# First norm, memory norm and memory keys/values as a lane beside the compression; semaphores cleared in the next block; last stores from two queues

## What is computed

```
u    = rms_norm(x, norm_g[0])                       # 1056 x 1024, input of one large projection (u @ w_in)
mkv  = rms_norm(mem_prompt, mem_norm_g) @ w_mkv     # 256 x 1024 @ 1024 x 512, an output, read later by cross-attention
kc,vc = compress(k, v of the page cache)            # sparse attention: blocks of 32 rows through a small MLP, 8 sequences + the prompt
rms_norm(x, g) = x * rsqrt(mean(x*x) + 1e-6) * g
```

## Time and profile before

| | us |
|---|---|
| three runs | 3834.92, 3834.66, 3845.22 (median 3834.92) |
| the profiled execution, whole | 3842.91 |
| its span in the trace | 3841.1 |
| PE busy | 3306.4 (86%) |
| blocks before the first merged stage (nm, memory_kv, n0) | 0 to 88.2 |
| first merged stage (36 dense units and the compression) | 88.2 to 476.4 |
| mean TensorE clock granted | 0.917 |

### The profile page before, as it was taken

How to read it: one execution, slowest core, us unless ns; L and a number is a source line. 1 busy time by engine, 2 the same in 40 slices (tenths; PEclk the granted TensorE clock), 3 DMA queues, 4 the chain that set the end, 5 groups by cost and what they waited for, 6 DMA issues and landing times. The chain is left out here.

```text
span 3841.1 us, 40240 instructions
## 1 busy us (share of the span) xinstructions
PE 3306.4 (86%) x14082; PEld 2043.6 (53%) x14082; DVE 1115.2 (29%) x2789; ACT 729.8 (19%) x1746; POOL 397.0 (10%) x296
## 2 busy tenths in 40 slices
PE   4799967778999968887999957989869999997998
PEld 2567745555556645544554535545546666663443
DVE  2011101111453315843555523313322232230000
ACT  1011100000221112322333322014411111111000
POOL 0010000000321003411000011001101101100000
PEclk7799988889997879998999978979989999998999
DMA  3333233232774226784001134420011111104000
GB/s 109 89 95 87 61 98 103 79 104 64 221 228 130 82 80 194 259 281 123 30 29 34 42 85 130 144 82 24 28 45 37 41 33 36 41 22 152 23 32 14
DMA packets 340509, 345.19 MB, mean 90 GB/s; under 512 B 54529, under 2 KB 311265, under 8 KB 339126
## 3 DMA queue, kind: packets, MB, share of 16 engines
q1 hardware_dynamic: 330002, 285.16, 24.5%
q10 hardware_dynamic: 10334, 57.82, 4.4%
HBM read 289.57 MB, written 110.01 MB: 104 GB/s over the span
## 5 line engine op out<-in xcount | busy, mean ns | idle before, releaser
L243 PE MATMUL d_ps<-d_w,mixer_u_T 128*128 128x288 f32 (+4 forms) x2304 | 723.9, 451 | 57.9 <-ACT d_ob L263 29.9
L2795 PE MATMUL ffn_ps<-up_u_T,ffn_w 128*128 128x352 f32 x2112 | 632.4, 461 | 0.0
L243 PEld LDWEIGHTS d_ps<-d_w,mixer_u_T 128*128 128x128 f32 (+1 forms) x2304 | 408.6, 192 | 227.3 <-issue 86.0
L2795 PEld LDWEIGHTS ffn_ps<-up_u_T,ffn_w 128*128 128x128 f32 x2112 | 400.4, 190 | 220.2 <-issue 1.2
L247 PE MATMUL d_ps<-mixer_u_T,d_w 128*128 128x352 f32 x1152 | 428.4, 497 | 44.4 <-PEq L86 40.0
L2676 PE MATMUL down_ps<-down_w,feed_g_T 128*128 128x512 f32 (+1 forms) x792 | 343.1, 596 | 17.6 <-DMA down_w<-ffn_w_down 17.6
L247 PEld LDWEIGHTS d_ps<-mixer_u_T,d_w 128*128 128x128 f32 x1152 | 206.6, 199 | 152.9 <-issue 89.2
L2676 PEld LDWEIGHTS down_ps<-down_w,feed_g_T 128*128 128x128 f32 (+1 forms) x792 | 144.4, 183 | 215.8 <-issue 197.9
L263 ACT COPY d_ob<-d_ps 128x288 f32<-128x288 f32 (+3 forms) x144 | 59.8, 417 | 662.6 <-PE d_ps L243 451.0
L2855 DVE TENSOR_SCALAR ffn_c<-ffn_h,ffn_now 128x1072 f32<-128x1072 f32 x44 | 36.9, 838 | 449.3 <-ACT ffn_h L2823 449.3
L2821 ACT COPY ffn_h<-ffn_ps 128x352 f32<-128x352 f32 x132 | 58.6, 444 | 526.7 <-PE ffn_ps L2795 526.7
(11 more groups left out here) (443 smaller groups left out, 3418.4 us busy)
## 6 DMA issues: line engine op xcount, KB each, us to landing
out_dil_sample<-cache_dil_w ACTq DMA_DIRECT2D x8, 4088.0 KB
ffn_w<-ffn_w_up SPq DMA_DIRECT2D x44, 512.0 KB, 4.7
cmp_rows<-cache_nsa_kv SPq DMA_DIRECT2D x128, 128.0 KB
graw<-d_ob SPq DMA_DIRECT2D x72, 176.0 KB, 1.9
mix_gate<-graw SPq DMA_DIRECT2D x24, 528.0 KB, 6.2
dils_qb<-proj SPq DMA_DIRECT2D x24, 512.0 KB, 7.2
d_w<-w_in SPq DMA_DIRECT2D x24, 512.0 KB, 5.6
ssd_x<-proj SPq DMA_DIRECT2D x29, 384.0 KB, 4.7
```

What stands on the lines that cost most here:

```text
L243: mm = pe.matmul(self.ps[u % 2][0:rows, 0:cols], self.u_T[:, k, r0:r0 + rows], self.view(i)[:, k, :], start=(k == 0), stop=(k == DK - 1))
L2795: mm = pe.matmul(ps[u][:, 0:chunk], w[:, slot, k, a, :], u_T[:, k, x * chunk:(x + 1) * chunk], start=(k == 0), stop=(k == DK - 1))
```

## The change

1. The blocks "nm", `memory_kv`, "n0" and the one that loads `ident` go. A new lane, `front_lane`, does their work in the first merged stage: nine tiles of x (F0 to F17, two halves a tile), two tiles of the memory (F18 to F21), and the 16 products of the memory's keys and values (F22 to F37). It has four input buffers and one PSUM bank (before four), so each half of the transposes waits for the copy of the half before. The dense lane waits (`ready`) for the tile that a unit of the first weight part reads.
2. The two output tiles of the compression share one PSUM bank, and the waits around them are for both tiles.
3. `Stage.__exit__` only notes its semaphores; POOL clears them at the beginning of the next block that calls `clear`, before its own work there (all `together` blocks, `combine_branches`, `ffn_up`, `project_out` and the last block; not `merge_branches`).
4. The last stores of nsas and dilp are issued half from SP and half from ACT.
5. The SSD's last states go to a buffer each (`h_raw`, whose content has been used by then, and `last_rows`), with no wait for stores in between.

```
@@ Stage
-        if self.sems and exc[0] is None:
-            with self.nc.Block() as block:
-                @block.gpsimd
-                def _(pool):
-                    for sem in self.sems:
-                        pool.sem_clear(sem)
-            for sem in self.sems:
-                self.nc.release_semaphore(sem)
+        Stage.used += self.sems
+def clear(nc, pool):
+    for sem in Stage.used:
+        pool.sem_clear(sem)
+        nc.release_semaphore(sem)
+    Stage.used = []
@@ together, combine_branches, ffn_up, project_out, last block
             @block.gpsimd
             def _(pool):
+                clear(nc, pool)
@@ Dense.lane, pe_program
                 if j == 0:
                     pe.wait_ge(self.w_in[i % 2], self.landed[i])
+                if ready is not None and i == 0:
+                    pe.wait_ge(ready, 2 * (j + 1))
@@ decoder_step
-            with Stage(nc, "cmp") as own:
-                together(nc, (dense.lane(36), 0, 0.8), (compress_lane(nc, own, ins, proj, kc_T, vc, ident), 0, 1))
+            with Stage(nc, "front") as own_f, Stage(nc, "cmp") as own:
+                normed = own_f.sem("normed")
+                front = front_lane(nc, own_f, ins, outs, u_T, x_rows, ident, ident_in, normed)
+                together(nc, (front, 0, 0.3), (dense.lane(36, ready=normed), 0.03, 0.82),
+                         (compress_lane(nc, own, ins, proj, kc_T, vc, ident), 0, 1))
@@ front_lane (new), its programs; copied is the semaphore "normed"
+    def pe_program(pe):
+        pe.wait_ge(ident_in, 16)
+        pe.wait_ge(gain_in, 32)
...
+        for t, (r0, m, _, _, _) in enumerate(tiles):
+            for j in range(2):
+                pe.wait_ge(scaled, 2 * t + 2)
+                if t or j:
+                    pe.wait_ge(copied, 2 * t + j)
+                for k in range(4):
+                    mm = pe.transpose(ps[:, k, 0:m], xt[0:m, t % RING, (4 * j + k) * P:(4 * j + k + 1) * P], ident[0:m, 0:m])
+                mm.then_inc(turned, 1)
+                yield
+        pe.wait_ge(w_in, 16)
+        pe.wait_ge(copied, 2 * own)
+        for t in range(MEM // P):
+            if t >= 1:
+                pe.wait_ge(kv_copied, t)
+            for k in range(DK):
+                mm = pe.matmul(ps[...], m_T[:, k, t * P:(t + 1) * P], w[:, k, :], start=(k == 0), stop=(k == DK - 1))
...
+    def act_program(act):
+        def root(t):
+            m, s = tiles[t][1], t % 2
+            act.wait_ge(x_in[t % RING], 16 * (t // RING + 1))
...
+            act.activation(junk[0:m, :], xt[0:m, t % RING, :], ACT.Square, accum_out=ss[0:m, 0, s:s + 1]).then_inc(squared, 1)
+            act.wait_ge(meaned, t + 1)
+            act.activation(ss[0:m, 2, s:s + 1], ss[0:m, 1, s:s + 1], ACT.Sqrt).then_inc(rooted, 1)
+        root(0)
+        for t in range(own):
+            if t + 1 < own:
+                root(t + 1)
+            yield
+            yield
+    def dve_program(dve):
+        def scale(t):
...
+            dve.tensor_scalar(xt[0:m, t % RING, :], xt[0:m, t % RING, :], ss[0:m, 3, s:s + 1], None, ALU.mult).then_inc(scaled, 1)
...
+        scale(0)
+        for t, (r0, m, _, out_T, g) in enumerate(tiles):
+            if t + 1 < own:
+                scale(t + 1)
+            for j in range(2):
+                dve.wait_ge(turned, 2 * t + j + 1)
+                dve.tensor_tensor(out_T[:, 4 * j:4 * j + 4, r0:r0 + m], ps[:, :, 0:m],
+                                  wide(gcol[:, g, 4 * j:4 * j + 4], m), ALU.mult).then_inc(copied, 1)
+                yield
...
+    def sp_program(sp):
+        load(0)
+        sp.dma_start(ident[:, :], ins["k_ident"]).then_inc(ident_in, 16)
+        sp.dma_start(grow[:, 0, :], ...).then_inc(gain_in, 16)
+        sp.dma_start(grow[:, 1, :], ...).then_inc(gain_in, 16)
+        for t in range(1, RING):
+            load(t)
+        yield
+        for t in range(own):
+            if t >= 1 and t - 1 + RING < own:
+                sp.wait_ge(turned, 2 * t)
+                load(t - 1 + RING)
+            if t == n - 2:
+                sp.dma_start(w[:, :, :], ins["w_mkv"]...).then_inc(w_in, 16)
+            yield
+            yield
...
+    return Lane((2 * own) + DK * (MEM // P), pe_program, act_program, dve_program, None, sp_program)
@@ dil_prompt_lane
-    def store(sp, n, sems):
+    def store(eng, n, sems, part, parts):
...
+        for ps, ts, rows in folded(o_dil[g, 0:SEQ, pair], d)[part::parts]:
+            eng.dma_start(rows, out[ps, s, ts, :]).then_inc(sems["stored"], 16)
+    def last_stores(act, sems):
+        store(act, n_rounds - 1, sems, 1, 2)
         elif n == n_rounds * per_round:
-            store(sp, n_rounds - 1, sems)
+            store(sp, n_rounds - 1, sems, 0, 2)
@@ compress_lane
-    O = [st.ps(f"O{i}", [P, P]) for i in range(2)]
+    both = st.ps("O", [P, 2, P])
+    O = [both[:, s, :] for s in range(2)]
-                    pe.wait_ge(outs_copied, (n - 1) * 2 + s + 1)
+                    pe.wait_ge(outs_copied, n * 2)
-                dve.wait_ge(outs_made, n * 2 + s + 1)
+                dve.wait_ge(outs_made, n * 2 + 2)
@@ ssd
-                if b >= 2:
-                    act.wait_ge(s_stored[b % 2], 32 * (b // 2))
-                act.copy(rows[:, b % 2], R[b % 2][:, 0:2, :]).then_inc(s_copied, 1)
+                act.copy(h_raw[:, b] if b < DB else last_rows[:, :, :], R[b % 2][:, 0:2, :]).then_inc(s_copied, 1)
@@ nsa_sample_lane (ACT, and SP after its last load)
+            store(act, b, range(BS if b + 1 < NB else BS // 2))
+            else:
+                sp.wait_ge(normalised, b + 1)
+                store(sp, b, range(BS // 2, BS))
```

## The result

The changed kernel took 3778.1 us (median of four runs, 3768.6 to 3793.4) against 3834.8 beside it, so the medians are 56.7 us apart. The ratio on record for the series is 0.9838, with a 95% interval of 0.9812 to 0.9865: 62 us less, by 10 either way. A second series gave 0.9853 (0.9818 to 0.9888). I had predicted 3769 (3747 to 3801).

What follows compares the result with a forecast made beforehand. PE was taken to bound the first stage from 141.1 to 476.4 us, but not the front ahead of it. Front 28.8, clearing 16.6, stores 7.6 and 5.0, SSD 8 sum to 66.0 us: 3769 us, range 3747 to 3801.

Steps and rivals of the forecast that it cites:

- First gather: Front of the merged stage: SP issues the first page gather at 19 us, 5.3 of it for added tiles.
- C1: Front: transposes of the first sequence start at 59 us, 40.1 after the first gather, PE idle till then.
- Tile 4: Front: its load stands behind 32 gathers on SP, lands 3.2 us after issue; PE, at F7 about 75, waits to 93.1.
- Tile 8: Front: its load stands behind 16 gathers, lands 2.1 us after issue; F15 at 135.8 after an 8 us PE wait.
- From C8 to the end: Rest of the first merged stage: from C8 at 141.5 to 447.6 us, 13.7 for the memory's 16 products.
- Clearing: Stage ends: 23.2 us of SP waits go, 6.6 come back at SSD, combination and last block; net -16.6 us.
- Stores: Last stores of sampled NSA and dilated stages from two queues: -7.6 and -5.0 us, if issue is the limit.
- SSD: End of the SSD stage: no store waits, cache copy issued about 5 us earlier; -8 us (0 to -10).
- B: Rival, 14%: single PSUM bank and in-order queues eat half of the front's gain; +25 us, 3794.
- C: Rival, 6%: two DMA issuers don't add up; the store parts give 3 us instead of 20.6; 3787.
- D: Rival, 4%: slower than before; SP bounds the merged stage if a gather rises from 2.04 to over 2.55 us; 3838 at 2.6.
- A: Rival, 15%: lanes fit better, earlier first gather, no wait at F15, more from SSD and clearing; 16 to 20 us more, 3751.

Runs made afterwards that it cites:

- the kernel with one queue: The changed kernel with the last stores of the sampled NSA and dilated stages each issued from one queue again: ratio 0.9891 to the kernel before.
- the three kernels with the shorter front alone: Changed kernel with tiles from ACT's queue (3765.5 us); also compression's turns later, memory weights from ACT (3752.1); also gathers right behind the page table, compression's weights from ACT (3740.6).
- the last one: The changed kernel with all edits that helped a stage: three front edits, memsets ahead of clearing, five cache copies moved to the prompt's NSA stage: 3724.4 us, ratio 0.9687.
- two with the front as changed: The changed kernel with last stores from one queue (ratio 0.9891), and with memsets ahead of the clearing in SSD and combination (ratio 0.9841).

## Why the prediction was right, and where it was off

Every wait that I named came where I named it, and the median was 9 us above the forecast. The sizes that were wrong cost some 13 us, a tile's landing behind the gathers and the tail of the SSD above all, and nothing large came in to make them good: the medians show 57 us where I had 66. Step by step:

- *First gather* 19, measured 21.61; *C1* 59, measured 63.60. Here I took 5.3 us for the added tiles; they cost 8.
- *Tile 4*: PE reached F7 at 75.7 (predicted 75) and waited as foreseen, but to 101.99, not 93.1. The step that failed is "the tile lands 3.2 us after its issue": it took 9.1. That landing time came from a stretch with one tile under way; here three went out together with 1.3 MB of weights behind 32 gathers. Another 3.3 came from the later first gather and the pitch (2.10 us a gather for 2.08).
- *Tile 8*: F15 at 146.69 against 135.8. Nine of that are inherited; landing was 5 us after issue, not 2.1. PE's wait was 11.75 (predicted 8). The table load took 1.28 us, with the next instruction 0.01 behind, so the trace sides again with the row and not with the 2.66 of the Trainium skill, "ScalarE: Activation LUTs", section "What ACT_TABLE_LOAD costs".
- *From C8 to the end*: 304.5 us against 306.1 predicted, 1.2 of which is clearing that is gone, and no stall on `rows_T` but one of 1.1 us. So the sum holds, but not each of its terms: the memory's 16 products took 16.7 us of PE time (32 instructions), not 13.7, and the others were not taken apart. The front's miss of 9.4 us (455.9 for 446.4) lies ahead of C8, which came 9.8 late.
- *Clearing*: 14.6 of 15.0 in the stages that can be compared, with the tail's 5.6 read from its end (12.2 by stage lengths alone). Only the FFN's 1.5 was too much: 0.3 came, since PE's work in the stage took 1.2 longer, with a slower clock at its start. The two waits that come back, 3.4 and 2.3, were exact as SP's waits (5.2 less 1.8, 2.5 less 0.2).
- *Stores* 7.6 and 5.0: 6.4 and 5.1. The dilated stage seemed to give 2.0 more, since the series began 1.7 us after SP's last dense store, not 3.6. But in the second profile of the kernel before it began 1.7 after it too, so these 2.0 are no part of the change: 9.0 came for the 8.8 of clearing and stores together.
- *SSD* -8 for the stores: 4.3, by the SSD stage with the clearing undone (326.6) against 331.0 (338.5 in the second profile of before, so the size is not sharp). The PE wait of 3.0 went as foreseen; the term that was mis-sized is the tail. With the clearing undone the last copy was issued 301.2 us into the stage, 3.2 earlier than before (304.5) and not 5; in the changed kernel it was at 305.0, since the clearing's 3.4 stand at the stage's start. Behind the copy I had counted on a tail some 3 us shorter, and it was 1.1 shorter (25.4 us to the next stage for 26.5): the copy filled the DMA engines, and the stores behind it stayed slow. So it came out between my -8 and "0 if the copy stays where it is".

Of the rivals, B's single PSUM bank did not show: PE's waits for the lane's copies other than F7's and F15's are 1 us in all. B's in-order queue did in part, as 12 us more than the 26 priced at F7 and F15. C is refuted by the stages of the kernel with one queue, D by the gathers' pitch (2.01 to 2.10 us). Of A, nothing came. One of my signs of being wrong came up: the stages behind 476 changed by 54.1 us in the two profiles, not 37. Without the dilated stage's 16.2 and 2.0 it is 35.9.

Not settled: why the granted clock in the dilated stage falls to 0.50 (1.2 GHz) some 220 us after its start, for 10 to 60 us, and in most profiles again from about 350 us on, and what makes it long or short; whether a shorter front makes it longer (in the three kernels with the shorter front alone PE took 423, 418 and 435 us there, but 395 in the last one and 422 in two with the front as changed); why the FFN's clock rises later; and the 7.5 us between the two SSD stages of the kernel before.

## What to carry to other kernels

When work is moved into a merged order, follow each in-order queue that issues its loads, and take landing times from a stretch that is as full as the new one will be. A small load behind a long series of DMA issues costs the whole series; another engine's queue gives it its place back, though it then shares the DMA engines with what runs there. Where the clock's spread is larger than the effect, read the effect from stages that repeat, or from the time between PE's last product and the next stage's first DMA, which repeated within 0.1 us at most stage ends here.

## What the runs showed of the hardware

- Two queues issuing together were each a little slower than one alone in the sampled NSA stage: ACT's 12 stores took 8.5 us and SP's 8.9, 0.71 and 0.74 each, against 0.63 each (24 in 15.1) from one queue. In the dilated stage they hardly were: eight took 5.0 and 5.2 us, 0.62 and 0.65 each, against 0.63.
- The landing of a 512 KB tile was 3.2 us alone, 5.6 and 10.1 beside page gathers, and 9.5 with two more tiles and 1.3 MB of weights (medians).
- The time between PE's last product and the next stage's first DMA was the same within 0.1 us at the tail's end in all ten profiles without clearing blocks (1.60 to 1.61) and in all three with them (7.17 to 7.25), while the stage's length moved by 2.7.
- The same 1755 PE instructions took from 393 to 435 us in thirteen profiles of eleven programs, with a mean granted clock of 0.93 to 0.84. Whole executions of the kernel before took 3824 to 3868 us, at a mean clock of 0.921 to 0.911.
